# A new order of all steps in the Gated DeltaNet stage of a two-block network on one core

## The chip, the cores and the metric

The program runs on one NeuronCore of a Trainium2 chip. Five engines work side by side and each takes its own list of instructions in order: TensorE (PE: matmuls and transposes; PEld: the loads of their stationary operand), VectorE (DVE), ScalarE (ACT), GpSimd (POOL) and SyncE (SP, which issues DMAs). They wait for each other only through semaphores. The metric is the device time of one execution in microseconds, lower is better. Before, the median of 3 runs is 1462.04 us (1458.76 to 1465.81).

## The reference, cut to what matters

A network on 256 tokens of width 1024 in float32: two layers of attention mixers (`block0`, `block1`), then, as the second part, FFN, short convolution, FFN, FFN, Gated DeltaNet ("Gdn"), FFN. The change touches the Gdn stage alone:

```python
proj = x @ w_in                                    # 1024 -> 2*1024 + 2048 + 2048 + 32
qkv, z, b, a = split(proj)
qkv = silu(causal_depthwise_conv(qkv, conv_w))     # width 4
q, k = l2norm(q), l2norm(k)                        # 8 heads of 128, each used by 2 of 16 value heads
beta, g = sigmoid(b), -exp(a_log) * softplus(a + dt_bias)
# per chunk of the gated delta rule: g = cumsum(g), decay = exp(g_i - g_j) below the diagonal
a = strict_lower((k * beta) @ k.T * decay)
t_inv = inverse(eye + a)
u, w = t_inv @ (v * beta), t_inv @ (k * beta * exp(g))
v_new = u - w @ state
o = (q * exp(g)) @ state + causal(q @ k.T * decay) @ v_new
state = state * exp(g_last) + k_tail.T @ v_new
...
o = o * rsqrt(mean(o * o) + eps) * norm_w * silu(z)
return o @ w_out                                   # 2048 -> 1024
```

The kernel takes 128 tokens as one chunk, which gives the same result.

## The kernel before, in words

Every large matmul is done to nearly float32 accuracy with three passes: a weight arrives as `raw`, ScalarE rounds it to `w_hi` (`split_hi`, L209), VectorE makes `w_lo = raw - w_hi` (`split_lo`, L227), and TensorE adds `x_hi*w_hi`, `x_hi*w_lo` and `x_lo*w_hi` (L245 to L247). Weights come in "units" of 1 MB, through a ring of four slots; SyncE loads a unit when the one four before it has been used (`Walk.load`, L194). So a unit needs its load, two halves `hi` on ScalarE, two halves `lo` on VectorE, and TensorE waits for the second `lo`.

The stages follow one another in the plan block0, block1, ffn00, conv, ffn01, ffn10, gdn, ffn11. In the Gdn stage (class `Gdn`) all engines read one list written out by hand, `GDN_ORDER`: every engine walks it from the top and issues, of each step, its own part. The list so fixes the order on each engine at once, and what an engine doesn't take part in it skips. The steps:

- `first:k0` and `unit:c:h:q`: a quarter (6 matmuls of 128x512) of weight unit h of chunk c. Chunks are k0, ba, k1, q0, q1, v0 to v3, z0 to z3, each 512 columns of the projection (ba: 32). `out:h:q`: a quarter (6 matmuls) of the output projection; its units 6 and 7 come after the list, in `last_units`. Units are numbered for `hi:n:half` and `lo:n:half`: k1 is 3 and 4, v1 11 and 12, v2 13 and 14, z3 23 and 24, `out:h` is 25 + h.
- `evac:c:t`: ScalarE takes a chunk's result for 128 tokens out of the two banks (L2489; `evac:ba:0` L2485). The next chunk's matmuls into that bank wait for it.
- `conv:c:p`: TensorE turns half a chunk (4 transposes, L2290), ScalarE and VectorE do the taps (L2537, L2702). `silu` is three ScalarE passes (L2544 to L2546) between two of VectorE. `l2` squares on ScalarE (L2550), `norm` sums them with a matmul against ones (L2298) and scales. All of these, with `kk`, `qk`, `vt`, `ba` and `ot`, share the two banks A2 and A3, and each waits until the last user of its bank has been read.
- `kk`, `kd`: the decayed products of keys of one key head (L2309, L2312; L2751). `blocks`, `gather`, `solved`, `spread`: SyncE moves the 16x16 diagonal blocks to DRAM and back, GpSimd inverts them in between; 0 is for key heads 0 to 3, 1 for 4 to 7.
- `core:g:x`: key head g. `k1` (L2382), `x2` (L2389), `t2` (L2396, L2401), `x1` (L2408), `t1`, `x0` (L2422), `t0` (L2427) build the inverse of the whole chunk from that of the blocks, with 16 to 56 matmuls on tiles of 32 or 64 or some transposes; `p0` to `p4` (L2433 to L2458) apply it and carry the state. Between two such steps of one head stands an instruction of ScalarE or VectorE on its result (`t2` on VectorE: 7 instructions, L2837). Heads run in pairs, on two sets of banks.
- `z1`, `z2`: gate and norm of the output on ScalarE and VectorE; `ot:n` turns it (L2352) and splits it into `o_hi` (L2594) and `o_lo` (L2816).

A line of the list is, by its layout, one quarter and what follows it. What TensorE does in a line behind its quarter is called a place with small steps here: there are 83 in the list.

Of the kernel before, what the change touches and what calls it, by code (L numbers as in the profile page):

```python
# [1847 lines left out]


GDN_ORDER = """  # L1850
    first:k0 evac:k0:0
# [3 lines left out]
    unit:ba:0:3 evac:ba:0 hi:4:1 hi:5:0 hi:5:1 silu:k0:0:0 silu:k0:1:0 lo:4:0 lo:4:1 lo:5:0 hi:6:0 silu:k0:0:1
        silu:k0:1:1 l2:k0:0
    unit:k1:0:0
    unit:k1:0:1 hi:6:1
    unit:k1:0:2
    unit:k1:0:3 lo:5:1  # L1860
    unit:k1:1:0 ba:t
    unit:k1:1:1 evac:k1:0 ba:0
    unit:k1:1:2 lo:6:0 norm:k0:0
    unit:k1:1:3 evac:k1:1 l2:k0:1 lo:6:1
    unit:q0:0:0 conv:k1:0
    unit:q0:0:1 hi:7:0 norm:k0:1
    unit:q0:0:2 hi:7:1 ba:1
    unit:q0:0:3 silu:k1:0:0 lo:7:0 kk:0:0 kk:0:1
    unit:q0:1:0 kd:0:0 lo:7:1 kd:0:1 conv:k1:1 hi:8:0 hi:8:1
    unit:q0:1:1 evac:q0:0 hi:9:0  # L1870
    unit:q0:1:2 kk:1:0
    unit:q0:1:3 kk:1:1 kd:1:0 evac:q0:1 silu:k1:0:1
    unit:q1:0:0 kd:1:1 silu:k1:1:0
    unit:q1:0:1 lo:8:0 kk:2:0 kk:2:1 kd:2:0 hi:9:1 silu:k1:1:1 kd:2:1
    unit:q1:0:2
    unit:q1:0:3 hi:10:0 hi:10:1 lo:8:1 kk:3:0 kk:3:1 kd:3:0
    unit:q1:1:0 l2:k1:0 l2:k1:1 lo:9:0 kd:3:1 ba:2
# [3 lines left out]
    unit:v0:0:0 evac:q1:1 conv:q0:1
    unit:v0:0:1 hi:11:0 hi:11:1
    unit:v0:0:2
    unit:v0:0:3 hi:12:0 hi:12:1 silu:q0:0:0 silu:q0:1:0 lo:11:0 silu:q0:0:1 lo:11:1 l2:q0:0
# [6 lines left out]
    unit:v1:0:2
    unit:v1:0:3 lo:13:0 lo:13:1
    unit:v1:1:0 kk:4:0
    unit:v1:1:1 kk:4:1 kd:4:0
    unit:v1:1:2 evac:v1:0 silu:q1:0:1
    unit:v1:1:3 kd:4:1 hi:14:1 evac:v1:1 hi:15:0 silu:q1:1:0 lo:14:0 lo:14:1
    unit:v2:0:0 kk:5:0
    unit:v2:0:1 kk:5:1 kd:5:0 core:0:k1
    unit:v2:0:2 core:1:k1
# [7 lines left out]
    unit:v3:0:2 silu:v0:0:1 core:1:x0
    unit:v3:0:3 vt:v0:0 core:0:x0 lo:16:0 silu:v0:1:1 vt:v0:1 lo:16:1 lo:17:0 lo:17:1 conv:v1:0 hi:18:0 core:0:t0
    unit:v3:1:0 core:1:t0 conv:v1:1 ba:3
    unit:v3:1:1 evac:v3:0 core:0:p0  # L1910
    unit:v3:1:2 hi:18:1 core:1:p0
    unit:v3:1:3 kk:6:0 kk:6:1 evac:v3:1 hi:19:0 kd:6:0 lo:18:0 core:0:p1 kd:6:1 core:1:p1 hi:19:1
    unit:z0:0:0 silu:v1:0:0 silu:v1:1:0 qk:1
    unit:z0:0:1 silu:v1:0:1 core:1:p2 core:0:p2 kk:7:0 kk:7:1 kd:7:0 lo:18:1
    unit:z0:0:2 core:1:p3 core:0:p3
    unit:z0:0:3 kd:7:1 core:1:p4 hi:20:0 core:0:p4 blocks:1
    unit:z0:1:0 vt:v1:0 silu:v1:1:1 vt:v1:1 z2:z0:0 lo:19:0 lo:19:1
    unit:z0:1:1 conv:v2:0 core:2:k1 core:3:k1 gather:1
    unit:z0:1:2 conv:v2:1 evac:z0:0 core:2:x2 core:3:x2
    unit:z0:1:3 hi:20:1 evac:z0:1 hi:21:0  # L1920
# [3 lines left out]
    unit:z1:0:3 silu:v2:0:1 silu:v2:1:1 vt:v2:0 core:2:x1 vt:v2:1 lo:20:0 lo:20:1 core:3:t1 core:2:t1 lo:21:0
        lo:21:1 conv:v3:0 solved:1 hi:22:0 core:3:x0
    unit:z1:1:0 hi:22:1 lo:22:0 lo:22:1 core:2:x0
    unit:z1:1:1 conv:v3:1 core:3:t0 core:2:t0 evac:z1:0
    unit:z1:1:2 spread:1 core:2:p0 core:3:p0
    unit:z1:1:3 hi:23:0 evac:z1:1
    unit:z2:0:0 qk:2  # L1930
# [7 lines left out]
    unit:z3:0:0 core:4:x1 hi:24:1 hi:25:0 z2:z1:0
    unit:z3:0:1 core:5:x1 core:4:t1
    unit:z3:0:2 core:4:x0 z1:z1:1 lo:24:0 lo:24:1 core:5:t1  # L1940
    unit:z3:0:3 core:5:x0
    unit:z3:1:0 z2:z1:1 hi:25:1 core:5:t0 core:4:t0
    unit:z3:1:1 z1:z1:2 hi:26:0 z2:z1:2 core:4:p0 ot:1 core:5:p0
    unit:z3:1:2 lo:25:0 ot:2 core:4:p1 ot:3 core:5:p1 lo:25:1
    unit:z3:1:3 evac:z3:0 evac:z3:1 hi:26:1 core:4:p2 core:5:p2
    out:0:0 core:4:p3 core:5:p3 z2:z2:0
    out:0:1 hi:27:0 lo:26:0 core:4:p4 core:5:p4
    out:0:2 hi:27:1 core:6:k1 core:7:k1
    out:0:3 lo:26:1 core:6:x2 core:7:x2 z1:z2:0 z1:z2:1 z2:z2:1 lo:27:0
# [3 lines left out]
    out:1:3 core:6:t1 core:7:x0 z2:z2:2 lo:28:0 lo:28:1 core:6:x0
    out:2:0 core:6:t0 hi:29:1 core:7:t0 core:6:p0
    out:2:1 core:7:p0
    out:2:2 core:6:p1 core:7:p1
    out:2:3 z1:z3:0 lo:29:0 core:6:p2 core:7:p2
    out:3:0 core:7:p3 core:6:p3
    out:3:1 hi:30:0 lo:29:1 hi:30:1 z2:z3:0 core:7:p4 core:6:p4
    out:3:2 lo:30:0 ot:4 z1:z3:1 lo:30:1  # L1960
    out:3:3 ot:5
# [1065 lines left out]
```

How the kernel before makes its waits and increments, by code:

```python
    def sync(self):  # L47
        self.eng.wait_ge(self.sem, self.n)
# [130 lines left out]
    def load(self, dst_dims, src):  # L179
        u, net = self.u, self.net
        if u >= RING:
            self.eng.wait_ge(net.unit_used, u - RING + 1)
        k, m = dst_dims[0], dst_dims[-1]
        for piece in range(2):
            if len(dst_dims) == 2:
                assert k % 2 == 0
                dst = net.raw[:, u % RING, piece * k * m // 2:(piece + 1) * k * m // 2]
                dst = dst.rearrange("p (k n) -> p k n", k=k // 2)
                part = src[:, piece * k // 2:(piece + 1) * k // 2, :]
            else:
                dst = net.raw[:, u % RING, 0:k * 2 * m].rearrange("p (k g n) -> p k g n", k=k, g=2)[:, :, piece, :]
                part = src[:, :, piece, :]
            self.eng.dma_start(dst, part).then_inc(net.raw_full[u % RING], 16)
        self.u += 1
# [1 line left out]
    def split_hi(self, half=None, half_done=None):  # L197
        net, v, act = self.net, self.u, self.eng
        self.u += half != 0
        if v >= len(net.sizes):
            return
        n = net.sizes[v]
        part = slice(n // 2 if half == 1 else 0, n // 2 if half == 0 else n)
        act.wait_ge(net.raw_full[v % RING], 32 * (v // RING + 1))
        if v >= RING:
            act.wait_ge(net.unit_used, v - RING + 1)
        ins = act.activation(net.w_hi[:, v % RING, part], net.raw[:, v % RING, part], ACT.Copy)
# [199 lines left out]
    def gain(self, dve, n):  # L409
        tt, h = self.groups[n]
        dve.wait_ge(*self.turned(n + 1))
        if n >= 2:
```

## Time and profile before

| | |
|---|---|
| median of 3 runs | 1462.04 us (1458.76 to 1465.81) |
| the profiled execution, its own time | 1464.56 us |
| its span | 1462.5 us |
| mean granted TensorE clock | 0.994 |
| PE busy | 1429.1 us (98%), 8043 matmuls |
| PEld busy | 1168.3 us (80%) |
| DVE busy | 1011.5 us (69%) |
| ACT busy | 839.1 us (57%) |
| POOL busy | 90.0 us (6%) |
| the Gdn stage | about 979.5 to 1264 us of the span |

A busy share is the time with an instruction in flight. Matmuls overlap each other, and their ends are modelled, so the distance of two starts says more than a length. In rows of a timeline, "x4" is a group of instructions in a run, the bracket is the engine's idle time before it and what ended it; "issue" means that nothing the profile shows did.

### The profile page before, as it was taken

The numbers are of one execution on the slowest core, as the hardware profiler recorded it, in microseconds if no ns is written. First come the engines' busy times: TensorE is split into PE (matmuls) and PEld (weight loads), VectorE is DVE, ScalarE is ACT, GpSimd is POOL, SyncE is SP. The second block draws the span as 40 slices with busy tenths as digits, with TensorE's granted clock in tenths as the row PEclk, the third lists the DMA queues.
The fourth block names the chain that finished last, engine by engine and source line by source line (L and its number), as shares of the span: only waits on it lengthen the run. The fifth ranks groups of instructions, "written<-read, shape, count | busy, mean of one in ns | idle before, by whom it ended". The sixth has DMA issues, their size and how long they took to land. (4 is left out here: it accounts for less than half of the span.)

```text
span 1462.5 us, 20277 instructions
## 1 busy us (share of the span) xinstructions
PE 1429.1 (98%) x8043; PEld 1168.3 (80%) x8043; DVE 1011.5 (69%) x1397; ACT 839.1 (57%) x1250; POOL 90.0 (6%) x170
## 2 busy tenths in 40 slices
...
GB/s 226 184 116 116 156 178 109 112 106 199 195 178 197 173 190 171 186 191 183 200 174 180 197 184 187 187 159 176 123 152 101 117 88 95 151 202 184 191 186 101
DMA packets 164189, 237.73 MB, mean 163 GB/s; under 512 B 17714, under 2 KB 110544, under 8 KB 164096
## 3 DMA queue, kind: packets, MB, share of 16 engines
...
q8 instruction: 64, 1.05, 0.3%
...
q10 hardware_dynamic: 64, 0.02, 0.0%
...
## 5 line engine op out<-in xcount | busy, mean ns | idle before, releaser
L227 DVE TENSOR_TENSOR w_lo<-raw,w_hi 128x1024 fp32r<-128x1024 f32 (+2 forms) x296 | 509.1, 1742 | 178.1 <-ACT w_hi L209 177.5
L209 ACT ACTIVATE w_hi<-raw 128x1024 fp32r<-128x1024 f32 (+2 forms) x296 | 428.1, 1461 | 181.3 <-DMA raw<-in_ffn_w_gate_up 140.3
L245 PE MATMUL A<-w_hi,x_hi 128*128 128x512 f32 (+1 forms) x640 | 263.4, 412 | 8.6 <-DVE w_lo L227 3.0
L247 PE MATMUL A<-w_hi,x_lo 128*128 128x512 f32 (+1 forms) x640 | 249.9, 390 | 0.0
L246 PE MATMUL A<-w_lo,x_hi 128*128 128x512 f32 (+1 forms) x640 | 249.2, 389 | 0.0
L245 PEld LDWEIGHTS A<-w_hi,x_hi 128*128 128x128 f32 x640 | 121.8, 190 | 41.0 <-DVE x_lo L419 8.3
L247 PEld LDWEIGHTS A<-w_hi,x_lo 128*128 128x128 f32 x640 | 121.6, 190 | 25.7
L246 PEld LDWEIGHTS A<-w_lo,x_hi 128*128 128x128 f32 x640 | 122.1, 191 | 20.9 <-issue 0.7
L245 PE MATMUL A<-w_hi,ffn_ffn_hT_hi 128*128 128x512 f32 x352 | 138.8, 394 | 0.0
L246 PE MATMUL A<-w_lo,ffn_ffn_hT_hi 128*128 128x512 f32 x352 | 138.5, 393 | 0.0
L662 ACT ACTIVATE ffn_ffn_e<-ffn_ffn_z 128x512 f32<-128x512 f32 x44 | 27.8, 632 | 192.2 <-DVE ffn_ffn_z L696 192.2
L247 PE MATMUL A<-w_hi,ffn_ffn_hT_lo 128*128 128x512 f32 x352 | 137.4, 390 | 0.0
L245 PE MATMUL M<-w_hi,x_hi 128*128 128x512 f32 x320 | 126.7, 396 | 0.0
L245 PE MATMUL G<-w_hi,x_hi 128*128 128x512 f32 x320 | 126.7, 396 | 0.0
L247 PE MATMUL M<-w_hi,x_lo 128*128 128x512 f32 x320 | 125.0, 390 | 0.0
L247 PE MATMUL G<-w_hi,x_lo 128*128 128x512 f32 x320 | 124.9, 390 | 0.0
L246 PE MATMUL G<-w_lo,x_hi 128*128 128x512 f32 x320 | 124.7, 390 | 0.0
L246 PE MATMUL M<-w_lo,x_hi 128*128 128x512 f32 x320 | 124.7, 390 | 0.0
L703 DVE TENSOR_TENSOR ffn_ffn_gs<-ffn_ffn_z,ffn_ffn_e 128x512 f32<-128x512 f32 x44 | 30.5, 692 | 81.0 <-ACT ffn_ffn_e L664 81.0
L247 PEld LDWEIGHTS A<-w_hi,ffn_ffn_hT_lo 128*128 128x128 f32 x352 | 66.1, 188 | 14.8
L245 PEld LDWEIGHTS A<-w_hi,ffn_ffn_hT_hi 128*128 128x128 f32 x352 | 66.1, 188 | 14.6
L246 PEld LDWEIGHTS A<-w_lo,ffn_ffn_hT_hi 128*128 128x128 f32 x352 | 66.3, 188 | 13.1
...
## 6 DMA issues: line engine op xcount, KB each, us to landing
...
```

Source lines behind the costliest of these rows:

```text
L209: ins = act.activation(net.w_hi[:, v % RING, part], net.raw[:, v % RING, part], ACT.Copy)
L227: ins = dve.tensor_tensor(net.w_lo[:, v % RING, part], net.raw[:, v % RING, part], net.w_hi[:, v % RING, part].bitcast(F32), ALU.subtract)
L245: pe.matmul(out, xh, hi[:, k, c, :], start=start and k == 0, stop=False)
L246: pe.matmul(out, xh, lo[:, k, c, :], start=False, stop=False)
L247: mm = pe.matmul(out, xl, hi[:, k, c, :], start=False, stop=stop and k == nk - 1)
L662: w.chain(act.activation(self.e[:, :, :], self.z[:, :, :], ACT.Exp, scale=-1.0))
L703: w.chain(dve.tensor_tensor(self.gs[:, :, :], self.z[:, :, :], self.e[:, :, :], ALU.mult))
```

## The change

`GDN_ORDER` is replaced. Both lists hold the same 507 steps; no step is added, dropped or altered, and no other line of the kernel changes. The new list was sought by a program with random delays on each instruction. It has small TensorE steps in 72 places in place of 83 (one of these behind `first`, not counted). The lines that the prediction speaks of:

```diff
-    first:k0 evac:k0:0
-    unit:ba:0:0 evac:k0:1 conv:k0:0
-    unit:ba:0:1
-    unit:ba:0:2 hi:4:0 conv:k0:1
-    unit:ba:0:3 evac:ba:0 hi:4:1 hi:5:0 hi:5:1 silu:k0:0:0 silu:k0:1:0 lo:4:0 lo:4:1 lo:5:0 hi:6:0 ...
+    first:k0 evac:k0:0 evac:k0:1 conv:k0:0
+    unit:ba:0:0 conv:k0:1 hi:4:0 hi:4:1 evac:ba:0
+    unit:ba:0:1 hi:5:0 silu:k0:0:0
+    unit:ba:0:2 hi:5:1
+    unit:ba:0:3 silu:k0:1:0
...
-    unit:q1:1:1 evac:q1:0 blocks:0 lo:9:1 lo:10:0 lo:10:1
-    unit:q1:1:3 conv:q0:0 gather:0
+    unit:q1:1:1 evac:q1:0 lo:9:1 ba:2 blocks:0 lo:10:0 hi:10:1 l2:k1:1 lo:10:1
+    unit:v0:0:2 gather:0 hi:12:0 hi:12:1
...
-    unit:v0:1:3 l2:q0:1 lo:12:1 norm:q0:0 norm:q0:1 conv:q1:0 solved:0 evac:v0:1
-    unit:v1:0:0 conv:q1:1 hi:13:0 hi:13:1 hi:14:0
-    unit:v1:0:1 spread:0 silu:q1:0:0
+    unit:v0:1:3 norm:q0:0 norm:q0:1 conv:q1:0 conv:q1:1 hi:13:0
+    unit:v1:0:3 solved:0
+    unit:v1:1:2 silu:q1:0:1 spread:0 kd:4:0 kd:4:1 evac:v1:0
...
-    unit:v2:0:3 silu:q1:1:1 kd:5:1 hi:15:1 lo:15:0 lo:15:1 core:0:x2 l2:q1:0 l2:q1:1
-    unit:v2:1:0 core:0:t2 core:1:x2 norm:q1:0 core:1:t2 norm:q1:1 core:0:x1 conv:v0:0 hi:16:0
-    unit:v2:1:1 conv:v0:1 hi:16:1 core:1:x1
+    unit:v2:0:3 hi:15:1 lo:15:0 core:1:k1 lo:15:1 l2:q1:1 core:0:x2 norm:q1:0 core:1:x2 core:0:t2 norm:q1:1
+    unit:v2:1:0 core:1:t2 hi:16:0 conv:v0:0 conv:v0:1
+    unit:v2:1:1 core:0:x1 evac:v2:0 core:1:x1 evac:v2:1 hi:16:1
...
-    unit:z1:0:0 silu:v2:0:0 silu:v2:1:0 core:3:t2
-    unit:z1:0:1 hi:21:1 core:2:t2
-    unit:z1:0:2 core:3:x1
+    unit:z1:0:0 core:3:x2 evac:z0:1 hi:21:1 silu:v2:0:0 silu:v2:1:0
+    unit:z1:0:1 lo:20:0 core:2:t2 core:3:t2
+    unit:z1:0:2 core:2:x1 silu:v2:0:1 lo:20:1 silu:v2:1:1 core:3:x1
...
-    unit:z2:0:1 hi:23:1 core:2:p1 core:3:p1
-    unit:z2:0:2 silu:v3:0:0 silu:v3:1:0 lo:23:0 lo:23:1 core:2:p2 core:3:p2
-    unit:z2:0:3 core:3:p3 core:2:p3
-    unit:z2:1:0 silu:v3:0:1 silu:v3:1:1 z1:z0:0 z1:z0:1 z2:z0:1 qk:3 vt:v3:0 core:3:p4 core:2:p4
-    unit:z2:1:1 z1:z0:2 core:5:k1 core:4:k1 hi:24:0
-    unit:z2:1:3 z2:z0:2 evac:z2:0 evac:z2:1 core:4:t2 vt:v3:1 core:5:t2 ot:0
+    unit:z2:0:1 core:3:p1 lo:22:1 lo:23:0 lo:23:1 silu:v3:1:0 silu:v3:0:1
+    unit:z2:0:2 core:2:p2 core:3:p2 core:2:p3
+    unit:z2:0:3 core:3:p3 silu:v3:1:1 z1:z0:0
+    unit:z2:1:0 z2:z0:1 core:3:p4 qk:3 z1:z0:1 vt:v3:0 core:2:p4 hi:24:0 core:5:k1
+    unit:z2:1:1 core:4:k1 vt:v3:1
+    unit:z2:1:3 z1:z0:2 z2:z0:2 evac:z2:0 z1:z1:0 core:4:t2 core:5:t2 ot:0
...
-    out:1:0 core:7:t2 core:6:t2
-    out:1:1 core:7:x1 hi:28:0 hi:28:1 lo:27:1
+    out:1:0 core:7:t2 lo:27:1
+    out:1:1 core:6:t2 core:7:x1
...
-    out:4:3 z2:z3:1
-    out:5:0 z1:z3:2
-    out:5:1 hi:31:0 hi:31:1 hi:32:0 z2:z3:2 ot:6
-    out:5:2 ot:7
-    out:5:3 hi:32:1 lo:31:0 lo:31:1 lo:32:0 lo:32:1
+    out:4:1 hi:31:0 z2:z3:1 hi:31:1 lo:30:0
+    out:4:3 lo:30:1
+    out:5:0 z1:z3:2
+    out:5:1 z2:z3:2 lo:31:0 ot:6 hi:32:0 lo:31:1
+    out:5:2
+    out:5:3 hi:32:1 lo:32:0 ot:7 lo:32:1
```

## Rows read from the trace of the kernel before

**Rows 1.** Busy time by stretches: us, PE, PEld, DVE, ACT, POOL (instructions), PEclk, DMA.

```profile
1043.00:1100.00 57.00, 55.16 (x512) 42.43 (x511) 51.79 (x102) 44.90 (x80) 22.53 (x36) 1.00 0.48 140
...
sum 284.50, PE 274.32 PEld 220.27 DVE 231.97 ACT 207.15 POOL 56.46; mean PE 34.29 PEld 27.53 DVE 29.00 ACT 25.89 POOL 7.06
```

**Rows 2.** Waits of PE from 979.4 to 1264: us in total, times, longest.

```profile
PE A L245 <- DVE w_lo L227: 2.8, 2, 2.4
PE A L245 <- issue: 2.1, 1, 2.1
PE A L2298 <- ACT gdn_gd_sg L2550: 1.1, 1, 1.1
PE M L2382 <- DVE gdn_gd_v L2870: 0.9, 1, 0.9
...
PE A L245 <- ACT gdn_gd_u L2489: 0.6, 1, 0.6
PE M L2453 <- DVE gdn_gd_MT L2861: 0.6, 1, 0.6
PE A L245 <- ACT gdn_gd_D L2485: 0.5, 1, 0.5
```

**Rows 3.** Stretches again, PE alone: us, PE busy, PEclk, DMA share, GB/s.

```profile
1212.60:1216.00 3.40, 3.38 (x23) 0.51 0.03 8
...
1256.90:1260.30 3.40, 3.40 (x10) 0.50 0.31 109
```

**Rows 4.** Timeline of DVE, end of the stage: start, length, instruction, idle before it.

```profile
1250.76 0.75 DVE L2816 SCALAR_TENSOR_TENSOR x_lo<-G,cols,x_hi 128x512 fp32r<-128x512 f32 x1 [3.31 <-ACT x_hi L2594]
1252.52 0.75 DVE L2816 SCALAR_TENSOR_TENSOR x_lo<-M,cols,x_hi 128x512 fp32r<-128x512 f32 x1 [1.01 <-ACT x_hi L2594]
1253.19 6.82 DVE L227 TENSOR_TENSOR w_lo<-raw,w_hi 128x1024 fp32r<-128x1024 f32 x5
```

**Rows 5.** Timeline of PE around the wait for "issue".

```profile
1209.31 0.44 PE L2396 MATMUL M<-gdn_gd_U,gdn_gd_X 32*32 32x16 f32 x32
...
1209.84 0.43 PE L2396 MATMUL M<-gdn_gd_U,gdn_gd_X 32*32 32x16 f32 x31
...
1212.62 0.59 PE L245 MATMUL A<-w_hi,gdn_gd_o_hi 128*128 128x512 f32 x1 [2.08 <-issue]
```

**Rows 6.** The page: PE's instructions; a DMA queue's packets, MB, share.

```profile
PE 1429.1 (98%) x8043; PEld 1168.3 (80%) x8043; DVE 1011.5 (69%) x1397; ACT 839.1 (57%) x1250; POOL 90.0 (6%) x170
...
q8 instruction: 64, 1.05, 0.3%
```

**Rows 7.** DMA from 1210 to 1211.5: the instruction queue's packets, MB, share.

```profile
q8 instruction: 1, 0.02, 5.2%
```

**Rows 8.** Timeline of PE around a place that holds one `t2`.

```profile
1131.77 0.39 PE L246 MATMUL A<-w_lo,x_hi 128*128 128x512 f32 x1
1132.00 0.39 PE L247 MATMUL A<-w_hi,x_lo 128*128 128x512 f32 x1
...
1133.28 0.40 PE L246 MATMUL A<-w_lo,x_hi 128*128 128x512 f32 x1
```

**Rows 9.** Timelines of ACT and PE at the start of the stage.

```profile
992.41 1.27 ACT L2489 ACTIVATE gdn_gd_u<-A,small 128x512 f32<-128x512 f32 x2 [0.94 <-PE A L247]
995.23 1.06 ACT L209 ACTIVATE w_hi<-raw 128x1024 fp32r<-128x1024 f32 x1
...
993.15 0.30 PE L280 MATMUL A<-x_hi,w_hi 128*32 128x256 f32 x1 [0.78 <-ACT gdn_gd_u L2489]
```

**Rows 10.** Timeline of PE behind `norm:q1:1`.

```profile
1082.10 1.12 PE L2298 MATMUL A<-gdn_gd_sg,gdn_gd_ones 128*128 128x512 f32 x2
1083.35 0.44 PE L2408 MATMUL G<-gdn_gd_T,gdn_gd_MT 32*32 32x32 f32 x16
```

**Rows 11.** Timelines of POOL and PE: the first mask and `core:0:k1`.

```profile
1067.53 1.31 POOL L2100 TENSOR_TENSOR gdn_gd_ML<-gdn_gd_MT,level_f 128x512 f32<-128x512 f32 x1 [7.78 <-DMA gdn_gd_MT<-gdn_solved]
...
1073.78 0.60 PE L2382 MATMUL M<-ident,gdn_gd_U 128*128 128x128 f32 x4
```

More of the change, by code:

```diff
@@ L1850 @@
 GDN_ORDER = """
-    first:k0 evac:k0:0
-    unit:ba:0:0 evac:k0:1 conv:k0:0
-    unit:ba:0:1
-    unit:ba:0:2 hi:4:0 conv:k0:1
[L1855 to L1877, printed above, removed]
@@ L1878 @@
-    unit:q1:1:1 evac:q1:0 blocks:0 lo:9:1 lo:10:0 lo:10:1
-    unit:q1:1:2 norm:k1:0 norm:k1:1
-    unit:q1:1:3 conv:q0:0 gather:0
[L1881 to L1884, printed above, removed]
-    unit:v0:1:0
-    unit:v0:1:1 silu:q0:1:1 evac:v0:0 lo:12:0
-    unit:v0:1:2
-    unit:v0:1:3 l2:q0:1 lo:12:1 norm:q0:0 norm:q0:1 conv:q1:0 solved:0 evac:v0:1
-    unit:v1:0:0 conv:q1:1 hi:13:0 hi:13:1 hi:14:0
@@ L1890 @@
-    unit:v1:0:1 spread:0 silu:q1:0:0
[L1891 to L1899, printed above, removed]
-    unit:v2:0:3 silu:q1:1:1 kd:5:1 hi:15:1 lo:15:0 lo:15:1 core:0:x2 l2:q1:0 l2:q1:1
-    unit:v2:1:0 core:0:t2 core:1:x2 norm:q1:0 core:1:t2 norm:q1:1 core:0:x1 conv:v0:0 hi:16:0
@@ L1902 @@
-    unit:v2:1:1 conv:v0:1 hi:16:1 core:1:x1
-    unit:v2:1:2
-    unit:v2:1:3 evac:v2:0 evac:v2:1 hi:17:0 hi:17:1 silu:v0:0:0 qk:0
-    unit:v3:0:0 silu:v0:1:0 core:1:t1 core:0:t1
-    unit:v3:0:1
[L1907 to L1920, printed above, removed]
-    unit:z1:0:0 silu:v2:0:0 silu:v2:1:0 core:3:t2
-    unit:z1:0:1 hi:21:1 core:2:t2
@@ L1923 @@
-    unit:z1:0:2 core:3:x1
[L1924 to L1930, printed above, removed]
-    unit:z2:0:1 hi:23:1 core:2:p1 core:3:p1
-    unit:z2:0:2 silu:v3:0:0 silu:v3:1:0 lo:23:0 lo:23:1 core:2:p2 core:3:p2
@@ L1933 @@
-    unit:z2:0:3 core:3:p3 core:2:p3
-    unit:z2:1:0 silu:v3:0:1 silu:v3:1:1 z1:z0:0 z1:z0:1 z2:z0:1 qk:3 vt:v3:0 core:3:p4 core:2:p4
-    unit:z2:1:1 z1:z0:2 core:5:k1 core:4:k1 hi:24:0
-    unit:z2:1:2 core:5:x2 core:4:x2 z1:z1:0
-    unit:z2:1:3 z2:z0:2 evac:z2:0 evac:z2:1 core:4:t2 vt:v3:1 core:5:t2 ot:0
[L1938 to L1949, printed above, removed]
-    out:1:0 core:7:t2 core:6:t2
-    out:1:1 core:7:x1 hi:28:0 hi:28:1 lo:27:1
-    out:1:2 core:6:x1 z1:z2:2 core:7:t1 hi:29:0
@@ L1953 @@
[L1953 to L1961, printed above, removed]
+    first:k0 evac:k0:0 evac:k0:1 conv:k0:0
+    unit:ba:0:0 conv:k0:1 hi:4:0 hi:4:1 evac:ba:0
+    unit:ba:0:1 hi:5:0 silu:k0:0:0
@@ new lines @@
+    unit:ba:0:2 hi:5:1
+    unit:ba:0:3 silu:k0:1:0
+    unit:k1:0:0 lo:4:0
+    unit:k1:0:1 lo:4:1
+    unit:k1:0:2 ba:t silu:k0:0:1
+    unit:k1:0:3
+    unit:k1:1:0 lo:5:0 hi:6:0
+    unit:k1:1:1 l2:k0:0 lo:5:1 silu:k0:1:1 ba:0 evac:k1:0 lo:6:0 hi:6:1 evac:k1:1
+    unit:k1:1:2
+    unit:k1:1:3 norm:k0:0
+    unit:q0:0:0 lo:6:1 l2:k0:1 conv:k1:0 hi:7:0
+    unit:q0:0:1 norm:k0:1
+    unit:q0:0:2 hi:7:1 ba:1 silu:k1:0:0
+    unit:q0:0:3 lo:7:0 kk:0:0 kk:0:1 lo:7:1 kd:0:0 kd:0:1
+    unit:q0:1:0 conv:k1:1 silu:k1:0:1
@@ new lines @@
+    unit:q0:1:1
+    unit:q0:1:2 hi:8:0 kk:1:0 hi:8:1 evac:q0:0
+    unit:q0:1:3 kk:1:1
+    unit:q1:0:0
+    unit:q1:0:1 hi:9:0 evac:q0:1 kd:1:0 kd:1:1 silu:k1:1:0 lo:8:0 kk:2:0 kk:2:1 kd:2:0
+    unit:q1:0:2 kd:2:1 lo:8:1 l2:k1:0 hi:9:1
+    unit:q1:0:3 kk:3:0 kk:3:1 kd:3:0
+    unit:q1:1:0 kd:3:1 lo:9:0 silu:k1:1:1 hi:10:0
+    unit:q1:1:1 evac:q1:0 lo:9:1 ba:2 blocks:0 lo:10:0 hi:10:1 l2:k1:1 lo:10:1
+    unit:q1:1:2 norm:k1:0 evac:q1:1
+    unit:q1:1:3 norm:k1:1 conv:q0:0 hi:11:0
+    unit:v0:0:0 conv:q0:1 hi:11:1
@@ new lines @@
+    unit:v0:0:1
+    unit:v0:0:2 gather:0 hi:12:0 hi:12:1
+    unit:v0:0:3 silu:q0:0:0 lo:11:0 silu:q0:1:0 silu:q0:0:1 lo:11:1 l2:q0:0 evac:v0:0 silu:q0:1:1
+    unit:v0:1:0
+    unit:v0:1:1 lo:12:0 l2:q0:1
+    unit:v0:1:2 evac:v0:1 lo:12:1
+    unit:v0:1:3 norm:q0:0 norm:q0:1 conv:q1:0 conv:q1:1 hi:13:0
+    unit:v1:0:0 hi:13:1 hi:14:0
+    unit:v1:0:1 hi:14:1 silu:q1:0:0 lo:13:0 lo:13:1
+    unit:v1:0:2 kk:4:0
+    unit:v1:0:3 solved:0
+    unit:v1:1:0 kk:4:1
+    unit:v1:1:1
+    unit:v1:1:2 silu:q1:0:1 spread:0 kd:4:0 kd:4:1 evac:v1:0
@@ new lines @@
+    unit:v1:1:3 evac:v1:1
+    unit:v2:0:0 lo:14:0 hi:15:0
+    unit:v2:0:1 l2:q1:0 silu:q1:1:0 kk:5:0 kk:5:1 core:0:k1
+    unit:v2:0:2 silu:q1:1:1 kd:5:0 kd:5:1 lo:14:1
+    unit:v2:0:3 hi:15:1 lo:15:0 core:1:k1 lo:15:1 l2:q1:1 core:0:x2 norm:q1:0 core:1:x2 core:0:t2 norm:q1:1
+    unit:v2:1:0 core:1:t2 hi:16:0 conv:v0:0 conv:v0:1
+    unit:v2:1:1 core:0:x1 evac:v2:0 core:1:x1 evac:v2:1 hi:16:1
+    unit:v2:1:2 hi:17:0
+    unit:v2:1:3 silu:v0:0:0 silu:v0:1:0 qk:0 core:0:t1 core:1:t1 lo:16:0
```

46 lines of the change are left out of this document (45 added, 1 removed).

## The prediction

> **What bounds the kernel now.** I read the busy time by stretches of the Gdn stage first [rows 1]. Of 284.5 us TensorE has 274.3 us with a matmul in flight, VectorE 232.0 and ScalarE 207.2. TensorE is the bound, it walks its list in order, and the stage holds only some 10 us in which it stands still. The change alters neither the number nor the shape of any instruction, so the most it can give is: these 10 us, what the clock lost around them, and the cost of passing between weight matmuls and small steps. The waits of TensorE name the 10 us [rows 2]: one wait of 2.4 us for a `w_lo` half, one of 2.1 us of "issue" (nothing in the profile released it), and nine of 0.3 to 1.1 us, of which five of 0.5 us and more stand there and one, of 0.78 us, in rows 9. The granted clock is at 0.5 for 3.4 us in two stretches of the stage, and each follows one of the two long waits [rows 3]. The next longest idle, 1.1 us for `l2` [rows 2], lies between 1043 and 1100, at a full clock throughout [rows 1]. 0.5 is the lower of TensorE's two levels, 1.2 in place of 2.4 GHz; 3.4 us at half rate lose 1.7 us of work, so 3.4 us for both.
>
> **The change, part by part.** Terms are differences, negative is faster.
>
> (a) *End of the stage.* Before, VectorE does `ot:6` and `ot:7` and only then `lo:31` and `lo:32`: it stands idle 3.31 us before `ot:6` and 1.01 us before `ot:7`, and then runs five splits in a row, 6.82 us [rows 4]. TensorE has done `out:5:3` by then and waits the 2.4 us for `lo:31` [rows 2]. The new order puts `lo:31:0` ahead of `ot:6` and `lo:31:1` and `lo:32:0` ahead of `ot:7`; one split costs 6.82/5 = 1.4 us at most, so they fill 4.3 us of idle time and `lo:31` ends before `out:5:3` does. What is late next is `lo:32`, now behind `ot:7`: one split is left after it where there were four, and TensorE has 12 matmuls (2.7 us) to run before it needs it. The cover is thin; if it is missed it costs some 0.5 us. Also late could be `ot:6` on ScalarE, since `z2:z3:2` now comes behind `lo:30`; the 3.31 us of idle time cover that. I take -2.4 (bounds -2.4 and -1.4), and with the wait the clock stays up: -1.7.
>
> (b) *The "issue" wait.* It stands right behind two adjacent `t2` steps: the second starts 0.53 us after the first, and from its end nothing comes until 1212.62 [rows 5]. One `t2` is 56 matmuls and as many weight loads, 112 instructions; the pair is 224. The instruction queue moves 64 packets of 1.05 MB in all, 16 KB each [rows 6]; 8043 matmuls with as many loads are 251 instructions a packet, so this is TensorE's program coming in, a block of about 250 instructions each time. One such packet was under way between 1210.0 and 1211.5 [rows 7]. I read the wait as a block that was asked for too late, because the pair of `t2` uses up a whole block in about 1 us. The number of TensorE instructions ahead of this place is the same in both orders (all steps of cores 0 to 5, `ot:0` to `ot:3` and the same units), so the block ends at the same instruction. In the new order six weight matmuls (`out:1:1`) stand between `core:7:t2` and `core:6:t2`: 6 x 0.23 = 1.4 us [rows 8]. The wait shrinks from 2.1 to 0.7 us: -1.4 (bounds 0 and -2.1). At 0.7 us I expect no drop of the clock, as none follows 0.9 or 1.1 us: -1.7.
> The Trainium skill says in "Runtime: NRT & Kernel Launch", section "Instruction fetch mechanics", that instructions come in 16 KiB blocks of 256 and that crossing a block is mostly hidden. The trace agrees on the block and, in rows 5 and 7, not on the hiding. By that rule this wait is something else and stays: -6.4 in place of -9.5 below (a rival).
>
> (c) *Start of the stage.* `conv:k0:0` now stands ahead of `unit:ba:0:0`. It needs both evacuations of `k0`, which end at 992.41 + 1.27 = 993.68; the unit needed the first alone and went at 993.15 [rows 9]: +0.6 with the way to TensorE. Then `evac:ba:0` stands behind both halves of `hi:4` and not one; a half is 1.06 us [rows 9], and TensorE waits 0.5 us for this evacuation already [rows 2]. With the 0.4 us that its matmuls end later, that is +0.7. Behind it the second wait for `w_lo` (2.8 - 2.4 = 0.4 us [rows 2]) goes, since TensorE comes later and the split does not: -0.4. Together +0.9 (bounds 0 and +1.6).
>
> (d) *Waits in the middle.* `norm:q1:0` and `norm:q1:1` each stood just ahead of a `t2` or `x1` that wasn't ready; such a norm is 2 matmuls of 512 columns, 0.46 us at 0.23 each [rows 8], but the next step comes 1.25 us after the second norm begins [rows 10], so 0.8 us too late, and as much is put down for the first. Now `core:1:x2` and a whole unit lie between: -0.9 for both, with 0.7 us of wait left. `unit:v2:0:0` waited 0.6 us for `evac:v1:0`, which is now two places earlier on ScalarE: -0.6. `core:p3` waited 0.6 us for VectorE, `core:k1` 0.9 us [rows 2]: in the new order `lo:23` stands a unit ahead of `core:2:p2` on VectorE and no longer right before it, `core:3:p4` stands there ahead of `qk:3`, and TensorE has `qk:3` and `vt:v3:0` to do before `core:5:k1`: -1.5. The 1.1 us for `l2:q0:0` stays, as its three ScalarE passes per half are in the same order; adding `conv:q1:1` to that place makes TensorE wait for one more pass there and saves a place: 0. Together -3.0 (bounds 0 and -4.8: the four middle waits of rows 2, 3.2 us, and 1.6 us at the norms).
>
> (e) *New waits.* `core:3:x1` and `core:5:x1` now follow at once on the other core's `x1`, while VectorE's update after the second `t2` is still running; `core:1:p4` stands 0.4 us behind the evacuation that it needs. What ScalarE and VectorE do otherwise (`hi`, `lo`, `silu`, `z1`, `z2` moved by a few units) costs nothing while TensorE is the bound: they have 77 and 52 us of slack in the stage [rows 1]. If that cover fails in a place, the place costs its own delay. No row of before can show these; bounds 0 and the 4.8 us of the old middle waits; I take +1.4, nearer to nothing, because each of the three named is a part of one VectorE or ScalarE instruction.
>
> (f) *SP and GpSimd.* `gather:0`, `solved:0`, `spread:0`, `blocks:1` and `gather:1` move by two to five units; their 8 + 1 DMAs each now stand behind other weight loads. `spread:0` goes behind a load that waits for the end of `v1:0`, about 2 us later than it ran. GpSimd's masks follow its landing, 1067.53 before; a mask takes 1.31 us, core 0 needs two, so 1070.1, and `core:0:k1` came at 1073.78 [rows 11]: 3.7 us of cover. Cost 0; beyond it, one for one on TensorE.
>
> (g) *Fewer places.* 83 places with small steps become 72. A place that holds one `t2` takes 1.28 us from the last weight matmul ahead to the second behind [rows 8]; less two matmuls (0.46) and the `t2` itself (0.53 [rows 5]) its passage costs 0.29. 11 places: between 0 and -3.2. Some of those merged hold `x`, `t` steps as this one, as many hold 128-wide transposes: half of it, -1.6.
>
> Sum: -2.4 - 1.7 - 1.4 - 1.7 + 0.9 - 3.0 + 1.4 - 1.6 = -9.5 us. The profiled execution took 1464.56 us, which is 2.5 above the median of the runs, so 1455.1 there and **1452.5** as a median.
>
> **Rivals.**
> *The middle gives nothing.* The old waits go and as many come: VectorE is at 82% in this stage [rows 1], and merging places asks it for two cores' updates in a row. Then (d) is 0 and (e) up to its bound of 4.8, say 3.5: -2.4 - 1.7 - 3.1 + 0.9 + 3.5 - 1.6 = -4.4, 1457.6. For it: TensorE met these waits one behind another, and a wait that goes lets it reach the next one earlier. Against: after 1170 all chains come some us earlier together.
> *The "issue" wait stays*, and the clock drop with it, being no late block (above): -6.4, 1455.7. For it: rows 2 show it once, though there are four such pairs; against: the packet in rows 7.
> *Slower: blocks run out in more places.* The new order makes dense runs: `core:0:x2` to `core:0:t2` with `core:1:t2` one unit on, `core:2:t2` beside `core:3:t2`, `core:4:t2` beside `core:5:t2`. Each place costs 2.1 + 1.7 = 3.8 us if the block ends as badly as in rows 5. With the old one kept and three more: -6.4 + 11.4 = +5.0, 1467. It decides from the second new one on (7.6 against 6.4). Against: for cores 4 and 5 the order before had them in one place too, with a transpose step between, and rows 2 show no second "issue" wait.
>
> **How the numbers follow.** Forecast 58%, own range 1448 to 1457; the middle gives nothing 24%; the wait stays 10%; slower 8%. 0.5% is 7.3 us, about what a measurement of this kernel can tell, so faster means under 1454.7: 0.49 + 0.01 + 0.04 = 54%. Within: 0.09 + 0.23 + 0.06 + 0.03 = 41%. Slower: the rest of the last rival, 5%. Range: below, every wait of the stage and the larger passage cost, -2.4 - 3.4 - 2.1 - 4.8 - 3.2 = -15.9, 1446.1; above, past the first rival to 1461.
>
> **What would show it.** Right: no wait for `w_lo` before the last units and no half-clock stretch there (a); "issue" under 1 us, behind `core:6:t2` or inside it, clock at 1.0 (b); `unit:k1:0:0` later than before, with over 1 us of waits for `evac` (c); `core:5:k1` without a wait (d). Wrong: several "issue" waits, a wait of over 1 us on VectorE that rows 2 don't have, `lo:32` late, or waits of TensorE in the stage that still add up to 8 us.

## The result, and the profile after

| | before | after |
|---|---|---|
| median | 1460.79 us (4 runs, 1458.76 to 1465.81) | 1450.66 us (4 runs, 1450.01 to 1453.67) |
| ratio to before | | 0.9935, 95% interval 0.9917 to 0.9953 |
| profiled execution, its span | 1464.56 us, 1462.5 us | 1453.67 us, 1451.7 us |

The kernel is 10 us faster (7 to 12 by the interval); 1452.5 was predicted, in a range of 1446.1 to 1461. "Before" and "after" are the names of the two kernels here. Line numbers of the new one are two lower (`L2399` for `L2401`), since its list is two lines of text shorter.

To see where the time went I took the start of the first weight matmul of a quarter from each trace and cut the Gdn stage at points at which TensorE has done the same steps by both lists. All in us; the last part ends at the sixth of the eight quarters behind the list.

| kernel | stage starts | to `q0:0:2` | to `out:0:0` | to `out:4:0` | to the end | stage |
|---|---|---|---|---|---|---|
| before | 979.50 | 34.77 | 184.29 | 42.44 | 23.12 | 284.62 |
| after | 978.08 | 35.10 | 181.49 | 39.58 | 18.91 | 275.08 |
| difference | -1.42 | +0.33 | -2.80 | -2.86 | -4.21 | -9.54 |

So 9.5 of the 10.8 us between the spans are in the stage. The 1.4 us ahead of it are not the change's: no line there differs, and before had two stretches at half the clock there that are longer in sum, some 10 us, than the two of after, some 7 us. T2 apart (below), with none there, starts its stage 4.7 us earlier than before. First before, then after, TensorE by stretches (us, busy, granted clock, DMA share, GB/s):

```profile
226.00:229.50 3.50, 3.50 (x10) 0.51 0.28 107
314.80:321.70 6.90, 5.91 (x14) 0.51 0.11 39
```

```profile
81.50:85.00 3.50, 3.50 (x10) 0.51 0.04 16
317.00:320.50 3.50, 3.50 (x10) 0.51 0.00 0
```

The page of after in its first row, with the same instructions as before [rows 6], and the stage [rows 1], by the columns of those rows:

```profile
PE 1421.8 (98%) x8043; PEld 1165.1 (80%) x8043; DVE 1007.7 (69%) x1397; ACT 839.6 (58%) x1250; POOL 84.8 (6%) x170
```

```profile
978.20:1253.20 275.00, 268.51 (x2415) 218.57 (x2416) 228.08 (x462) 207.75 (x413) 51.42 (x88) 1.00 0.42 129
```

TensorE still is the bound, with 6.5 us of idle time in the stage where there were 10. Its waits there, for [rows 2]:

```profile
PE G L2406 <- DVE gdn_gd_U L2835: 1.7, 2, 1.0
PE A L2288 <- ACT gdn_gd_u L2487: 1.4, 1, 1.4
PE A L245 <- ACT gdn_gd_D L2483: 1.0, 1, 1.0
PE M L2380 <- POOL gdn_gd_U L2098: 0.6, 1, 0.6
PE M L2440 <- DVE gdn_gd_MT L2850: 0.5, 1, 0.5
PE A L2288 <- ACT gdn_gd_sg L2552: 0.5, 1, 0.5
PE A L2296 <- ACT gdn_gd_sg L2548: 0.5, 1, 0.5
...
PE M L2399 <- issue: 0.2, 1, 0.2
```

The two long waits of before are gone (`w_lo`) or down to 0.2 us ("issue"), and so are those of `core:p3`, `core:k1` for VectorE and the unit for `evac:v1:0`. In their place stand two `x1` (L2406), `conv:k0:0` and `evac:ba:0` at the start (L2288, L2483), a mask of GpSimd (L2380) and one `p1` (L2440). The stretches that were at half the clock [rows 3] are at the full one, behind `core:6:t2` and in the last units:

```profile
1208.90:1212.30 3.40, 3.40 (x54) 2.67 (x51) 2.03 (x9) 2.37 (x6) 0.00 (x0) 1.00 0.03 5
...
1246.00:1249.50 3.50, 3.50 (x17) 2.65 (x16) 3.41 (x4) 2.50 (x2) 0.00 (x0) 1.00 0.69 196
```

### The profile page after: what moved, and what is told of

Read it like the earlier page. It is cut to its first block, busy times and chain, and to the rows that moved or that the text cites. A ratio compares the mean times of both kernels' runs of the same rounds, so it can differ in the third digit from the quotient of the medians.

```text
span 1451.7 us, 20276 instructions
## 1 busy us (share of the span) xinstructions
PE 1421.8 (98%) x8043; PEld 1165.1 (80%) x8043; DVE 1007.7 (69%) x1397; ACT 839.6 (58%) x1250; POOL 84.8 (6%) x170
## 3 DMA queue, kind: packets, MB, share of 16 engines
q8 instruction: 64, 1.05, 0.3%
## 4 chain that ended last, share of the span: by engine, by line
PE 90%; DVE 4%; ACT 3%; DMA 2%; issue 1%; SPq 0%; POOL 0%; ACTq 0%; DVEq 0%
PE A L245 17%; PE A L246 16%; PE A L247 16%; PE M L245 5%; PE G L245 5%; PE M L247 5%; PE G L247 5%; PE G L246 5%; PE M L246 5%; PE A L1267 1%; PE G L1188 1%; PE G L1235 1%; PE M L623 1%; DMA raw<-in_ffn_w_gate_up 1%; DVE gdn_gd_t L2700 1%
```

## The experiments

Each is one kernel, timed in turn with the kernel before on the same chip; its stage is cut as above. Before's row and after's are those of the first table; the last column is the ratio to before in time with its interval.

| kernel | stage starts | to `q0:0:2` | to `out:0:0` | to `out:4:0` | to the end | stage | ratio |
|---|---|---|---|---|---|---|---|
| t2 apart | 974.79 | 34.79 | 185.39 | 39.94 | 21.46 | 281.58 | 0.9976 (0.9961 to 0.9990) |
| tail | 979.27 | 34.75 | 182.97 | 42.51 | 19.02 | 279.25 | 0.9965 (0.9951 to 0.9979) |
| before, shifted | 981.36 | 34.77 | 183.31 | 39.03 | 23.09 | 280.20 | 0.9998 (0.9983 to 1.0013) |
| after, shifted | 979.00 | 35.12 | 182.05 | 39.59 | 18.91 | 275.67 | 0.9950 (0.9935 to 0.9966) |
| middle | 979.22 | 34.79 | 180.76 | 42.46 | 23.13 | 281.14 | 0.9970 (0.9956 to 0.9984) |
| old start | 978.93 | 34.43 | 181.02 | 39.80 | 18.90 | 274.15 | 0.9940 (0.9922 to 0.9958) |
| `x1` later | 979.11 | 35.12 | 180.66 | 39.84 | 18.98 | 274.60 | 0.9917 (0.9898 to 0.9937) |
| better 1 | 976.24 | 34.45 | 180.68 | 39.58 | 18.89 | 273.60 | 0.9926 (0.9909 to 0.9943) |
| better 2 | 977.66 | 34.41 | 183.23 | 39.92 | 18.91 | 276.47 | 0.9952 (0.9936 to 0.9967) |
| after again | 980.61 | 35.11 | 181.62 | 39.74 | 18.90 | 275.37 | 0.9939 (0.9921 to 0.9957) |

**T2 apart.** The kernel before, with the place behind `core:7:t2` split:

```diff
-    out:1:0 core:7:t2 core:6:t2
-    out:1:1 core:7:x1 hi:28:0 hi:28:1 lo:27:1
+    out:1:0 core:7:t2
+    out:1:1 core:6:t2 core:7:x1 hi:28:0 hi:28:1 lo:27:1
```

> The kernel before, with one change: core:6:t2 stands behind the matmuls of out:1:1 and no longer right behind core:7:t2. Late block: TensorE's program comes in blocks, and the block that was late behind the two t2 is now asked for at the same instruction but needed 1.4 us later. The wait of 2.08 us falls to 0.2 to 0.7 us, now inside or behind core:6:t2, and the half-clock stretch of 3.4 us behind it goes; the stage ends some 3 us earlier (0.998 of the time before). Rival, the wait belongs to something else (a result of core:6 or of out:1:0 that the profile doesn't name): a wait of about 2 us stays somewhere between 1209 and 1216, the clock falls as before, the time is the same within 0.5 us.

The wait is 0.71 us and stands inside `core:6:t2`, six matmuls before its end (TensorE's timeline), and behind it the clock stays at 1.00:

```profile
1207.94 0.44 PE L2394 MATMUL M<-gdn_gd_U,gdn_gd_X 32*32 32x16 f32 x32
1208.22 0.36 PE L2399 MATMUL M<-gdn_gd_X,gdn_gd_U 32*32 32x16 f32 x18
1209.29 0.21 PE L2399 MATMUL M<-gdn_gd_X,gdn_gd_U 32*32 32x16 f32 x3 [0.71 <-issue]
```

```profile
1209.50:1213.00 3.50, 3.50 (x68) 1.00 0.02 5
```

Where it stands decides it. Before, TensorE had run `core:7:t2` and `core:6:t2`, 112 instructions each, 224 in all, when it stopped. Here it stops after the 112 of `core:7:t2`, the 12 of the unit and 100 of `core:6:t2`: 224 again (one load more had gone out in both). It is a place in TensorE's program, not a result that is late.

**Before, shifted, and after, shifted.** Matmuls without use ahead of TensorE's first own instruction move its whole program against the blocks:

```diff
+            for _ in range(112):          # 16 in the changed kernel
+                pe.matmul(net.M[1][0:32, 0:16], net.ident[:, 0:32], net.ident[:, 0:16], start=True, stop=True)
             pe.wait_ge(net.first_params, 16 * len(net.row_loads[1]))
```

> The kernel before, its list unchanged, with 112 matmuls of 32x16 without use (224 instructions with their loads) at the very start, where TensorE waits 7.3 us for its first DMA; so every later instruction of TensorE moves on by 224 within the 256 of a block. Late block: the two t2 of cores 7 and 6 still stand side by side, but the block that ends in them now ends elsewhere: counted in the trace of before, no stretch of the program then uses a block in less than about 5.7 us, so no wait for issue of over 0.3 us is left in the stage, the half-clock stretch at 1213 goes, the time falls by 3 to 4 us (0.998 or 0.997). Rival, two adjacent t2 stall TensorE by themselves: the wait of 2.08 us stays behind core:6:t2 and the time is unchanged.

> The changed kernel, its list unchanged, with 16 matmuls of 32x16 without use (32 instructions) at the very start, in TensorE's first wait. Late block: by the count in the trace of the changed kernel the block now ends where it is used up fastest: 3.1 us from the instruction that asks for it to the one that needs the next, at core:2:t2 and core:3:t2 (near 1132), against 4.7 without the extra; 4.4 us near 1172 against 6.1; 4.6 near 1205 as before. About 5 us are needed, so a wait for issue of 1.5 to 2 us comes up between 1129 and 1135 and one of some 0.5 us between 1171 and 1176, perhaps with a half-clock stretch: 2 to 4 us slower than the changed kernel. Rival: no wait for issue of over 0.3 us, the time of the changed kernel within 0.5 us.

One such call is two matmuls and two loads in the trace (x224), so the shifts are 448 and 64 instructions, not 224 and 32. In before, shifted, the same two `t2` stand side by side and the unit follows at once:

```profile
1210.73 0.43 PE L2394 MATMUL M<-gdn_gd_U,gdn_gd_X 32*32 32x16 f32 x31
1210.98 0.44 PE L2399 MATMUL M<-gdn_gd_X,gdn_gd_U 32*32 32x16 f32 x24
1211.35 0.50 PE L245 MATMUL A<-w_hi,gdn_gd_o_hi 128*128 128x512 f32 x1
```

No wait for "issue" is left in its stage, and the stretch from `out:0:0` to `out:4:0` is 3.4 us shorter. The rival (two adjacent `t2` stall by themselves) is out. The whole was not faster, against the expectation: the extra matmuls took 12.1 us where 7.3 us were free, and the first weight matmul came at 19.78 us, before at 13.41.

In after, shifted, a wait comes up where there was none, at the pair `core:2:t2`, `core:3:t2`. The expectation's figures were counted for a shift of 32, so for 64 only the place is to its credit; the second wait that it names, near 1175, did not come:

```profile
1132.43 0.42 PE L2394 MATMUL M<-gdn_gd_U,gdn_gd_X 32*32 32x16 f32 x31
1132.68 0.42 PE L2399 MATMUL M<-gdn_gd_X,gdn_gd_U 32*32 32x16 f32 x22
1135.45 0.20 PE L2399 MATMUL M<-gdn_gd_X,gdn_gd_U 32*32 32x16 f32 x2 [2.34 <-issue]
```

It cost far less than its length (182.05 against 181.49 us to `out:0:0`), since the waits of 1.05 us for `core:3:x1` and of 0.5 us for a `p1` behind it went: the results that they wait for came meanwhile.

**Tail.** The kernel before, with its last lines changed:

```diff
-    out:5:1 hi:31:0 hi:31:1 hi:32:0 z2:z3:2 ot:6
-    out:5:2 ot:7
-    out:5:3 hi:32:1 lo:31:0 lo:31:1 lo:32:0 lo:32:1
+    out:5:1 hi:31:0 hi:31:1 hi:32:0 z2:z3:2 lo:31:0 ot:6 lo:31:1
+    out:5:2
+    out:5:3 hi:32:1 lo:32:0 ot:7 lo:32:1
```

> The kernel before, with the last three lines of the list alone changed: lo:31:0 ahead of ot:6, lo:31:1 and lo:32:0 ahead of ot:7 on VectorE. Own theory: the wait of 2.4 us for w_lo ahead of the last two units goes and so does the half-clock stretch of 3.4 us, -4.1 us (0.997); the next stage starts as early behind the last unit as before. Rival, the splits only change who is late: ot:7 or lo:32:1 comes later by the splits put ahead of it, TensorE waits 0.5 to 1.5 us at the last units, and the gain is under 2.5 us.

The last part takes 19.02 us in place of 23.12: -4.1, all of the term, by these three lines alone. VectorE's timeline of after, for [rows 4], shows the five splits spread around the two `ot`, whose idle time is now 0.83 us and none (1.96 and 0.17 us in the tail's kernel):

```profile
1241.74 1.22 DVE L227 TENSOR_TENSOR w_lo<-raw,w_hi 128x1024 fp32r<-128x1024 f32 x1
1243.80 0.75 DVE L2814 SCALAR_TENSOR_TENSOR x_lo<-G,cols,x_hi 128x512 fp32r<-128x512 f32 x1 [0.83 <-ACT x_hi L2592]
1244.47 2.46 DVE L227 TENSOR_TENSOR w_lo<-raw,w_hi 128x1024 fp32r<-128x1024 f32 x2
1247.01 0.75 DVE L2814 SCALAR_TENSOR_TENSOR x_lo<-M,cols,x_hi 128x512 fp32r<-128x512 f32 x1
```

**Middle.** The kernel before, with the new list from `unit:q0:0:2` to `out:0:0`, its lines as in the change.

> The kernel before with the changed list between unit:q0:0:2 and out:0:0 alone (both lists have done the same steps at these two points); start and end of the stage as before. Own theory, the middle is worth something by itself: from unit:q0:0:2 to out:0:0 it takes 181 to 182 us, as in the changed kernel, where the list before took 183.0 to 185.4 in four profiles; -1 to -3.5 us in all, the wait for issue (2.1 us) and the one for w_lo (2.4 us) stay. Rival, the middle gives nothing: 183 us or more there, the time of before within 1 us.

180.76 us there, against 184.29, 185.39, 182.97 and 183.31 in four profiles of the old list: -3.2 of their mean, 184.0. The rival (the middle gives nothing) is out. The spread of 2.4 us under one list says how far a single pair of profiles may be trusted here. Four other profiles with the same new middle (the changed kernel twice, shifted, and with the old start) have 181.0 to 182.1. What the waits do is mixed: three old ones of 0.6 to 0.9 us go, and the two for `x1` and one of 0.6 for GpSimd's mask come. TensorE's waits in the stage, in part; the one for "issue" is still there, as it should be:

```profile
PE A L245 <- issue: 1.9, 1, 1.9
PE G L2406 <- DVE gdn_gd_U L2835: 1.7, 2, 1.0
```

**Old start.** The changed kernel with the first five lines of before:

```diff
-    first:k0 evac:k0:0 evac:k0:1 conv:k0:0
-    unit:ba:0:0 conv:k0:1 hi:4:0 hi:4:1 evac:ba:0
+    first:k0 evac:k0:0
+    unit:ba:0:0 evac:k0:1 conv:k0:0
...
```

> The changed kernel with its first five lines as before: conv:k0:0 behind unit:ba:0:0, evac:ba:0 ahead of hi:4:1. Own theory: the waits of 1.36 us for evac:k0 and of 1.02 us for evac:ba:0 fall back to 0.78 and 0.52 us, unit:k1:0:0 comes 1.1 us earlier after the start of the stage (18.0 in place of 19.1 us), and as the waits for w_lo in the k1 units are gone by the lines behind, 0.7 to 1.1 us of that is kept at unit:q0:0:2. Rival, the start is given back: TensorE, earlier, meets w_lo that isn't ready in the k1 units, and unit:q0:0:2 comes within 0.2 us of the changed kernel's 35.1.

`unit:k1:0:0` comes 18.03 us after the start of the stage, after had 19.09: the five lines cost 1.06 us. Of this 0.67 is kept at `unit:q0:0:2` and 0.9 at the end of the stage. In time the two can't be told apart.

**X1 later.** The changed kernel with `core:3:x1` and `core:5:x1` a quarter later:

```diff
-    unit:z1:0:2 core:2:x1 silu:v2:0:1 lo:20:1 silu:v2:1:1 core:3:x1
-    unit:z1:0:3 core:3:t1 core:2:t1 lo:21:0 vt:v2:0 vt:v2:1
+    unit:z1:0:2 core:2:x1 silu:v2:0:1 lo:20:1 silu:v2:1:1
+    unit:z1:0:3 core:3:x1 core:2:t1 vt:v2:0 core:3:t1 lo:21:0 vt:v2:1
...
-    unit:z3:0:0 core:4:x1 core:5:x1
+    unit:z3:0:0 core:4:x1
+    unit:z3:0:1 core:5:x1 evac:z2:1 lo:24:0 core:4:t1 z1:z1:1 lo:24:1
```

> The changed kernel with core:3:x1 and core:5:x1 one quarter later (and core:2:t1, core:3:t1, core:5:t1, core:5:x0 moved behind them to fit). Own theory on the new waits: both x1 waited for VectorE's update after the second t2 (1.05 and 0.66 us), a unit of 1.4 us now covers it, both waits go and the stage is 1.2 to 1.7 us shorter from z1 to out:0:0. Rival: the chain of heads 3 and 5 is as long as TensorE's work there, and the wait comes back at t1, x0 or p0 behind it: within 0.4 us of the changed kernel.

Half: from `unit:q0:0:2` to `out:0:0` it is 0.8 us shorter, the stage 0.5. Both waits for VectorE (1.7 us in after) are gone, and TensorE's waits now have these:

```profile
PE M L2399 <- issue: 0.6, 1, 0.6
...
PE A L2331 <- DVE gdn_gd_t L2721: 0.4, 1, 0.4
```

**Better 1 and 2, and after again.** Better 1 has both edits and `core:0:k1` a quarter later; better 2 also spreads the steps behind `v0:1:3`:

```diff
-    unit:v0:1:3 norm:q0:0 norm:q0:1 conv:q1:0 conv:q1:1 hi:13:0
-    unit:v1:0:0 hi:13:1 hi:14:0
+    unit:v0:1:3 norm:q0:0 hi:13:0
+    unit:v1:0:0 norm:q0:1 hi:13:1
+    unit:v1:0:1 conv:q1:0 hi:14:0
+    unit:v1:0:2 conv:q1:1 hi:14:1 silu:q1:0:0 lo:13:0 lo:13:1
...
```

> The changed kernel with the edits of the two runs before it together, and core:0:k1 a quarter later (it waited 0.56 us for GpSimd's mask). If the waits are separate, the gains add up: 0.7 to 1.1, 1.2 to 1.7 and 0.5 us, some 2.5 to 3.3 us below the changed kernel, about 1448. If the chains only hand them on, it is within 1 us of the changed kernel.

> The version better1 with one more edit: norm:q0:1, conv:q1:0 and conv:q1:1 behind v1:0:0, v1:0:1 and v1:0:2, one a quarter, where all four steps stood behind v0:1:3. There TensorE needs 4.25 us for what single steps need some 1.9 us for elsewhere, because each step waits until ScalarE has read the step two ahead out of the same bank. If units between them cover these waits, the stage is 1 to 2 us shorter than better1's 273.6 us, and the median about 1448. Rival: the q1 chain is late by what its steps were moved, and the wait comes back at kk:4, norm:q1 or core:0:x2; no gain against better1.

> The changed kernel once more, unaltered, beside the other kernels of this call: some 10 us below the kernel before (0.993), its stage 275 to 276 us.

Better 1 has the shortest stage, 1.5 us below after's two profiles of 275.08 and 275.37, half of what was expected. Its third edit brought little: TensorE waits 0.46 us for GpSimd's mask at `core:1:k1`, where it had waited 0.56 at `core:0:k1`. Its ratio to before and after's two overlap, as do their medians (1451.85 us of 4 runs against 1450.66 and 1453.40); no version is shown to beat the changed kernel. Better 2 missed, and its rival held: 2.9 us longer than better 1. The chain of q1 was what the place was for; it ends later, and TensorE waits for it further on, above all at `core:1:x1`:

```profile
PE G L2406 <- DVE gdn_gd_U L2835: 2.2, 2, 2.0
PE A L2307 <- DVE gdn_gd_t L2700: 0.8, 1, 0.8
```

**Groups together, groups apart.** One run each, read from its trace. The changed kernel with extra matmuls behind quarters that nothing waits in; apart:

```diff
+                for _ in range({(3, 3): 1, (4, 0): 1, (4, 1): 1}.get((h, q), 0)):
+                    for n in range(4):
+                        pe.transpose(net.M[1][:, 0:P], self.U[1][:, 1, :], ident[:, :])
+                for _ in range({(4, 2): 1, (4, 3): 1, (5, 0): 1}.get((h, q), 0)):
...
```

together `{(3, 3): 3}` and `{(4, 2): 3}`.

> The price of a place by itself, first half. The changed kernel with six groups of extra matmuls whose results nobody uses, where TensorE waits for nothing: three groups of four 128-wide transposes in one place behind out:3:3, and three groups of eight 32x32 matmuls (as an x1 step has) in one place behind out:4:2. Term (g) of the prediction holds a place to cost 0.29 us beyond its work, half of that on the mean of the merged ones. Rival, read from the single and double places of both lists: two ot steps cost the same in one place as in two, two x1 steps 0.2 us less. The length from out:3:3 to out:4:2 and from out:4:2 to out:5:1 is compared with the kernel of the same groups in six places.

> The price of a place by itself, second half: the same six groups, one in each of six places (three of transposes behind out:3:3, out:4:0 and out:4:1, three of 32x32 matmuls behind out:4:2, out:4:3 and out:5:0). By term (g) each stretch, having two places more, is 0.3 to 0.6 us longer than with the groups together. By the rival the stretch with transposes is the same within 0.1 us (or shorter), that with 32x32 matmuls 0.3 to 0.4 us longer.

From `out:3:3` to `out:4:2` the transposes take 5.53 us together and 5.48 apart (4.21 without them): a place of its own costs nothing. From `out:4:2` to `out:5:1` the 32x32 matmuls take 5.18 us together and 5.84 apart: 0.33 us for each of two more places. The starts of these quarters' first matmuls, together and then apart:

```profile
1238.01 0.39 PE L245 MATMUL A<-w_hi,x_hi 128*128 128x512 f32 x1
...
1239.47 0.95 PE L2371 MATMUL M<-gdn_gd_U,gdn_gd_MT 32*32 32x32 f32 x48
...
1243.19 0.39 PE L245 MATMUL A<-w_hi,x_hi 128*128 128x512 f32 x1
```

```profile
1238.81 0.48 PE L245 MATMUL A<-w_hi,x_hi 128*128 128x512 f32 x1
...
1240.38 0.44 PE L2371 MATMUL M<-gdn_gd_U,gdn_gd_MT 32*32 32x32 f32 x16
...
1244.65 0.50 PE L245 MATMUL A<-w_hi,x_hi 128*128 128x512 f32 x1
```

## Why the prediction was right, step by step

By stretches the terms were: start (c) +0.9, middle (d), (e) and (g) -3.2, pair (b) -3.1, end (a) -4.1. Measured: +0.33, -2.80, -2.86, -4.21. The sum, -9.5, came out to a tenth. The places and the mechanisms of (a) and (b) were right; that the sum is so close is luck. The middle of one list spreads over 2.4 us between profiles, (c) was off by 0.6, and in the middle the single terms were off by more and made up for one another. Ahead of the stage 1.4 us came from the clock, with which no term reckoned.

(a) Right in place and size, and shown by the tail alone. T2 apart shows the two parts singly: TensorE waits 2.44 us for `w_lo` there too, but the clock stays up, and the last part takes 21.46 us, 1.7 less than before (the clock) and 2.4 more than in the tail (the wait). That the clock falls behind such a wait is no rule (below).

(b) Right, and shown three ways: the wait moves with the count of instructions, goes when the program is shifted, and comes up elsewhere when the shift puts it there. The 0.7 us that I kept measured 0.2 in after, 0.5 in after again, 0.7 with the pair apart and nothing in better 1. The pair alone doesn't use up a block in 1 us, as I had it: the 256 instructions up to the late one took 2.9 us. The Trainium skill ("Runtime: NRT & Kernel Launch", section "Instruction fetch mechanics") has blocks of 256 instructions and a crossing that is mostly hidden. The counts below agree with the first; the second doesn't hold for this run of short matmuls, behind which 2.08 us stood open. The rival is out.

(c) The lines cost 1.06 us against the 0.9 of the term (old start): TensorE waits 1.36 us for `evac:k0`, where it waited 0.78 [rows 9], and 1.02 us for `evac:ba:0`, where it waited 0.5 [rows 2]. What I missed is that most of it is given back: besides the wait of 0.4 us for `w_lo` that I counted, the k1 units take 0.4 us less, so that +0.33 stays. The wait for `w_lo` didn't need the later start for that, as I had it: it is gone with the old start too. The split ends 24.1 us into the stage there, as in before, but `ba:t` now stands ahead of `unit:k1:1:0` and fills the time.

(d) and (e) As waits, these went as foretold at `core:p3`, `core:k1` and `evac:v1:0`. The 0.9 us at the two `norm` came out as 0.3: from `unit:v2:0:2` to `unit:v2:1:2`, which hold the same steps in both lists, 12.36 us before and 12.02 after. The 1.1 us for `l2:q0:0` was to stay; it became 0.5, and `conv:q1:1` in the same place brought 0.5 of its own. The new waits are larger than my +1.4: `core:3:x1` 1.05 and `core:5:x1` 0.66, as named, and 0.5 for a `p1` that I hadn't named, 2.2 in all. The first is over 1 us on VectorE, which I had put down as a sign of being wrong. `core:1:p4` cost nothing. All in all the waits that the profile names in the middle are even, 3.7 us before and 3.8 after, (f) included, where (d) and (e) without the `norm` had -0.7.

(f) Held at 0, cost 0.56: `core:0:k1` waits for GpSimd's mask. The cover of 3.7 us was used up from both sides. The mask starts at 1069.08, where it had started at 1067.53 [rows 11], since `spread:0` stands behind a weight load that goes out at 1061.84 only, and TensorE comes to `core:0:k1` at 1071.1 and not at 1073.8:

```profile
1069.08 1.30 POOL L2098 TENSOR_TENSOR gdn_gd_ML<-gdn_gd_MT,level_f 128x512 f32<-128x512 f32 x1 [9.21 <-DMA gdn_gd_MT<-gdn_solved]
```

(g) This is the term that was mis-sized. I took the price of a place from one that holds a `t2`, 0.29 us, and halved it for all 11. By the groups it is 0.33 us for 32-wide matmuls and nothing for 128-wide transposes; and of the places that went only two held `x` or `t` steps (27 became 25, by the two lists). So it is worth 0.7 us by this estimate, not 1.6. That leaves some 2 of the middle's 2.8 us outside both the named waits and the price of places. They are gone in certain stretches: the place `kk:3:0 kk:3:1` took 1.76 us beyond its quarter before and 0.82 after, of which the waits of before show 0.4, and from `unit:z2:1:0` to `unit:z3:0:0` it is 13.35 us before and 11.70 after, of which they show 0.9. That the rest is waits too, hidden inside the modelled lengths of rows, is a guess that no run tests, so the middle's gain is shown as a whole and its cause only in part.

The rivals: the middle gave something, the wait did not stay, and no second wait for "issue" came. The last is closer than the chance of 8% says: in after, shifted, the new list's pair `core:2:t2`, `core:3:t2` stalls for 2.3 us.
